# A hybrid decoder layer on one core: the memory of the output product is laid out anew, and the last token tile takes its contraction halves in another order

## What is computed

```
xn     = rmsnorm(x)
merged = gate0 * (att @ w_att_out) + gate1 * (ssm @ w_ssm_out) + gate2 * (mem @ w_mem_out)
h      = x + merged @ w_o                      # w_o is 1024 x 1024: "the output product"
hn     = rmsnorm(h)
h      = h + hier_moe(hn)                      # top-1 group of 4, then top-2 of its 8 experts
y      = rmsnorm_final(h)
```

## Time and profile before

| what | value |
|---|---|
| median of 3 runs | 1182.9 us (1180.64 to 1184.21) |
| the profiled execution | 1183.2 us, of which the span from first to last instruction is 1181.5 us |
| PE busy / weight loads | 1066.9 us (90%) / 761.1 us (64%) |
| DVE / ACT / POOL busy | 35% / 19% / 11% |
| DMA | 330.32 MB, mean 280 GB/s; 412 to 424 GB/s in most slices of the second half |

### The profile page before, as it was taken

How to read it: one execution, slowest core, us unless ns; L and a number is a source line. 1 busy time by engine, 2 the same in 40 slices (tenths; PEclk the granted TensorE clock), 3 DMA queues, 4 the chain that set the end, 5 groups by cost and what they waited for, 6 DMA issues and landing times.

```text
span 1181.5 us, 16647 instructions
## 1 busy us (share of the span) xinstructions
PE 1066.9 (90%) x6831; PEld 761.1 (64%) x6831; DVE 412.2 (35%) x869; ACT 227.1 (19%) x445; POOL 135.1 (11%) x153
## 2 busy tenths in 40 slices
PE   7999999999999999999999599987887787888885
PEld 6888888887888888878845355544444444444441
DVE  3993305926566655422543510100000000000003
ACT  4103021125232222410032201111101111111114
POOL 2113401003010100000010011110011111110100
PEclk9999999999999999999999799999999999999998
DMA  6771266434766645279084499999999999999974
GB/s 229 248 263 55 90 226 229 136 113 169 231 227 229 219 158 188 93 280 395 34 313 169 173 412 392 415 418 420 417 418 421 420 420 421 424 421 419 418 316 148
DMA packets 50812, 330.32 MB, mean 280 GB/s; under 512 B 9084, under 2 KB 12236, under 8 KB 37552
## 3 DMA queue, kind: packets, MB, share of 16 engines
q1 hardware_dynamic: 33760, 259.75, 54.9%
q0 software_dynamic: 15104, 63.85, 16.3%
q10 hardware_dynamic: 1872, 5.66, 1.3%
HBM read 319.18 MB, written 62.11 MB: 323 GB/s over the span
## 4 chain that ended last, share of the span: by engine, by line
PE 64%; DMA 31%; ACT 2%; issue 1%; DVE 1%; SPq 1%; POOLq 0%; ACTq 0%; DVEq 0%
DMA arena<-in_w 26%; PE bank L777 14%; PE bank L957 12%; PE bank L1308 8%; PE bank L1171 5%; PE bank L1333 4%; PE bank L1162 4%; DMA arena<-in_w_stream 2%; PE bank L1081 2%; PE bank L869 2%; PE bank L790 1%; PE bank L948 1%; PE bank L996 1%; PE bank L1017 1%; ACT arena L1588 1%
## 5 line engine op out<-in xcount | busy, mean ns | idle before, releaser
L1308 PE MATMUL bank<-arena 128*64 128x256 f32 x2048 | 261.3, 411 | 64.9 <-DMA arena<-in_w 64.8
L1308 PEld LDWEIGHTS bank<-arena 128*64 128x64 f32 x2048 | 160.2, 143 | 157.9 <-issue 51.0
L777 PE MATMUL bank<-arena 128*128 128x260 f32 x768 | 169.8, 383 | 0.6 <-DMA arena<-in_w_stream 0.6
L777 PEld LDWEIGHTS bank<-arena 128*128 128x128 f32 x768 | 145.5, 190 | 23.3 <-issue 1.0
L957 PE MATMUL bank<-arena 128*128 128x260 f32 x672 | 152.6, 384 | 1.7 <-DVE arena L1913 1.7
L957 PEld LDWEIGHTS bank<-arena 128*128 128x128 f32 x672 | 125.7, 190 | 22.0 <-DVE arena L1913 2.5
L2244 DVE TENSOR_TENSOR arena<-arena,bank 128x256 f32<-128x256 f32 x32 | 13.5, 421 | 326.7 <-ACT arena L1645 326.7
L1333 PE MATMUL bank<-arena 128*64 128x512 f32 x512 | 117.2, 600 | 3.9 <-DVE arena L2250 3.0
L733 POOL DMA_INDIRECT y_dram<-arena,scatter_rows x31 | 44.3, 1428 | 385.6 <-ACT arena L1661 355.2
L1333 PEld LDWEIGHTS bank<-arena 128*64 128x64 f32 x512 | 37.3, 138 | 64.9 <-issue 55.6
L1645 ACT ACTIVATE arena<-bank 128x256 f32<-128x256 f32 x32 | 12.3, 383 | 318.9 <-PE bank L1308 318.9
(11 more groups left out here) (356 smaller groups left out, 1123.8 us busy)
## 6 DMA issues: line engine op xcount, KB each, us to landing
arena<-in_w SPq DMA_DIRECT2D x95, 2048.0 KB, 35.7
arena<-in_w_stream SPq DMA_DIRECT2D x50, 512.0 KB, 5.1
out_sample_swa_k<-in_cache_swa_k POOLq DMA_DIRECT2D x8, 2047.0 KB, 9.6
out_sample_swa_v<-in_cache_swa_v POOLq DMA_DIRECT2D x8, 2047.0 KB, 10.0
arena<-in_cache_mem_v SPq DMA_DIRECT2D x8, 512.0 KB, 8.2
arena<-in_w_o SPq DMA_DIRECT2D x2, 2048.0 KB, 9.9
out_sample_swa_k<-in_cache_swa_k POOLq DMA_DIRECT2D x8, 511.0 KB, 5.9
out_sample_swa_v<-in_cache_swa_v POOLq DMA_DIRECT2D x8, 511.0 KB, 5.7
```

The lines of the kernel that those rows point to most:

```text
L777: last = pe.matmul(bank[:, 2 * u + h, 0:HALF], ring[u][:, k, :], x[:, k, h * HALF:(h + 1) * HALF], start=k == 0, stop=k == KT - 1)
L1308: last = pe.matmul(bank[64 * q:64 * q + CAP, 2 + u, part * FE // 2:(part + 1) * FE // 2], xgT[e // 2 % 2][:, k, 64 * u:64 * u + CAP], w[:, ...
```

## The change

The homes of the weights are laid out anew, so that a seventh home (75.25 KB) is free during the product. For that `xh` has two buffers where it had three, `hnb` one where it had two, `scrap` goes (the squares are written into `hnb`, which holds the normed rows of the tile before, so that ACT waits for their store, `hnst`, ahead of L1612), and `w_o` is loaded in four pieces, one after another, once the branch products are through. The last tile takes k = 4 to 7 for both halves of the columns first (quarters 0 and 1) and k = 0 to 3 after that (quarters 2 and 3); the second half of `w_o` is then free after quarter 1 (`wo_right`), and n = 7 is loaded into its place. In that tile `turn_half(i, 0)` stands behind quarter 3, and the right half's transposes use another bank. Matrix n = 8 is loaded after the last matmul of the product, n = 9 behind the first gather; n = 7 is no longer split. `gain_f` (512 KB) is loaded at the end of the weights where it was loaded ahead of the product.

```
-HOMES = (66, 107.25, 123.25, 139.25, 155.25, 171.25, 50, 91.25, 187.25, 30)
+HOMES = (59.25, 107.25, 123.25, 139.25, 155.25, 171.25, 75.25, 187.25, 91.25, 30)
...
-        w_o = [at(HOMES[6], 4, D), at(HOMES[8], 4, D)]
-        xh = [at(30 + 4 * i, D) for i in range(3)]
-        hnb = [at(42, D), at(MK + 16.25, D)]
+        w_o = [at(kb, D) for kb in (38, 42, 46, 50.25)] + [at(HOMES[7] + 4 * k, D) for k in range(4)]
+        xh = [at(30 + 4 * i, D) for i in range(2)]
+        hnb = at(MK + 16.25, D)
...
-            sp.dma_start(w_o[1], t["w_o"][:, 4:8, :]).then_inc(s["wo"], 16)
             sp.wait_ge(s["Sj"], KT)
-            sp.dma_start(w_o[0], t["w_o"][:, 0:4, :]).then_inc(s["wo"], 16)
-            sp.dma_start(gain_f, t["norm_f"].partition_broadcast(P)).then_inc(s["gainf"], 16)
-            for i in range(3):
+            for k0, n in ((0, 2), (2, 1), (3, 1), (4, 4)):
...
+                sp.dma_start(dst, src).then_inc(s["wo"], 16)
+            for i in range(2):
                 load_x(i)
...
-            for i in (3, 4):
-                sp.wait_ge(hacc[i % 3], 16)
-                sp.wait_ge(s["hn"], i - 2)
-                sp.wait_ge(s["ht"], 2 * (i - 2))
+            for i in range(2, NT):
+                sp.wait_ge(hacc[i % 2], 16 * (i // 2))
+                sp.wait_ge(s["hn"], i - 1)
+                sp.wait_ge(s["ht"], 2 * (i - 1))
                 load_x(i)
-                for n in ((2, 3, 4), (5,))[i - 3]:
+                for n in ((2, 3), (4, 5), (6,))[i - 2]:
                     load_weight(n // 3, n % 3)
...
+            sp.wait_ge(*later("wo_right", 1))
+            load_weight(2, 1)
             sp.wait_ge(s["wo_mm"], 2 * NT - 1)
-            load_weight(2, 0)
+            load_weight(2, 2)
+            sp.wait_ge(hnst, 16 * NT)
             for i in range(2):
-                sp.wait_ge(hnst[i], 16 * len(range(i, NT, 2)))
-            load_half(0)
-            for i in range(3):
-                sp.wait_ge(hacc[i], 16 * len(range(i, NT, 3)))
+                sp.wait_ge(hacc[i], 16 * len(range(i, NT, 2)))
             sp.wait_ge(s["ht"], 2 * NT)
             sp.wait_ge(s["xg"], 16)
-            load_half(KT // 2)
-            load_weight(2, 2)
             load_weight(3, 0)
             for n in range(NHOME, NLOAD):
                 wait_release(n // 3, n % 3)
                 load_weight(n // 3, n % 3)
 
+            sp.dma_start(gain_f, t["norm_f"].partition_broadcast(P)).then_inc(s["gainf"], 16)
...
-                for k in range(4 * (quarter % 2), 4 * (quarter % 2) + 4):
+                ks = list(range(4 * (quarter % 2), 4 * (quarter % 2) + 4))
+                opens, closes = quarter % 2 == 0, quarter % 2 == 1
+                if i == NT - 1:
+                    half, opens, closes = quarter % 2, quarter < 2, quarter >= 2
+                    ks = range(4, 8) if opens else range(4)
+                for k in ks:
...
-                if quarter % 2 == 1:
+                if closes:
                     last.then_inc(s["wo_mm"], 1)
+                elif i == NT - 1 and quarter == 1:
+                    last.then_inc(later_sem("wo_right"), 1)
...
                 out_rows(i, 2)
-                turn_half(i, 0)
+                if i < NT - 1:
+                    turn_half(i, 0)
                 slot_tokens(i - 2)
                 out_rows(i, 3)
+                if i == NT - 1:
+                    turn_half(i, 0)
                 rank(i - 1)
...
                 act.wait_ge(s["h"], 2 * i + 1)
-                act.activation(scrap[0][0:n, :], x[0:n, 0:512], ACT.Square, accum_out=stat[0:n, 32 + i:33 + i]
+                wait_from(act, hnst, 16 * i)
+                act.activation(hnb[0:n, 0:512], x[0:n, 0:512], ACT.Square, accum_out=stat[0:n, 32 + i:33 + i]
                                ).then_inc(s["hss"], 1)
...
                 act.wait_ge(s["rstd"], i + 1)
-                wait_from(act, hnst[i % 2], 16 * (i // 2))
-                act.activation(hnb[i % 2][0:n, :], x[0:n, :], ACT.Copy, scale=stat[0:n, 5 + i:6 + i]
+                act.activation(hnb[0:n, :], x[0:n, :], ACT.Copy, scale=stat[0:n, 5 + i:6 + i]
                                ).then_inc(s["hn"], 1)
```

More of the change, by code:

```diff
@@ L103 @@
 END_BANK = (0, 2, 4, 6, 0)
-SPLIT = tuple(16 if i == 7 else 0 for i in range(NHOME))
 LATE = 29
@@ L340, in build @@
         xgT = [at(XN + 8, KT, P), at(XN + 12, KT, P)]
-        hT = [at(XN + 16, 2, P), at(86, 2, P)]
-        xg = at(82, D)
-        gain_f = at(46, D)
+        hT = [at(XN + 16, 2, P), at(58.25, 2, P)]
+        xg = at(54.25, D)
+        gain_f = at(50.25, D)
         sg = [at(MK + 16.25 + i, FE // 2) for i in range(2)]
@@ L372, in build @@
         wld = [sem(f"s_wld{i}") for i in range(NHOME)]
-        rows_in = [sem(f"s_rows_in{i}") for i in range(3)]
-        hacc = [sem(f"s_hacc{i}") for i in range(3)]
-        hnst = [sem(f"s_hnst{i}") for i in range(2)]
+        rows_in = [sem(f"s_rows_in{i}") for i in range(2)]
+        hacc = [sem(f"s_hacc{i}") for i in range(2)]
+        hnst = sem("s_hnst")
         def h_back_in(T):
-            return (rows_in[T], 16 * (len(range(T, NT, 3)) + 1)) if T < 3 else \
+            return (rows_in[T], 16 * (len(range(T, NT, 2)) + 1)) if T < 2 else \
                 (kdec[T], 32 * len(range(T, NB, NSLOT)) + 16)
@@ L706, in _ @@
                 pool.wait_ge(s["h"], 2 * i + 2)
-                pool.dma_start(h_acc[T * P:T * P + n, :], xh[i % 3][0:n, :]).then_inc(hacc[i % 3], 16)
+                pool.dma_start(h_acc[T * P:T * P + n, :], xh[i % 2][0:n, :]).then_inc(hacc[i % 2], 16)
                 pool.wait_ge(s["hn"], i + 1)
-                pool.dma_start(t["hn_dram"][T * P:T * P + n, :], hnb[i % 2][0:n, :]).then_inc(hnst[i % 2], 16)
+                pool.dma_start(t["hn_dram"][T * P:T * P + n, :], hnb[0:n, :]).then_inc(hnst, 16)
             pool.wait_ge(s["xgclear"], 1)
+            pool.wait_ge(hnst, 16 * NT)
             for i in range(2):
-                pool.wait_ge(hnst[i], 16 * len(range(i, NT, 2)))
-            for i in range(3):
-                pool.wait_ge(hacc[i], 16 * len(range(i, NT, 3)))
+                pool.wait_ge(hacc[i], 16 * len(range(i, NT, 2)))
             def one_pass(p, late=0):
@@ L1169, in out_rows @@
                 T, half = ORDER[i], quarter // 2
-                for k in range(4 * (quarter % 2), 4 * (quarter % 2) + 4):
+                ks = list(range(4 * (quarter % 2), 4 * (quarter % 2) + 4))
[4 more added lines that the diff above has]
+                for k in ks:
                     last = pe.matmul(bank[:, 2 * (i % 2) + half, :], gates[:, k, T * P:T * P + P],
-                                     w_o[k // 4][:, k % 4, half * 512:(half + 1) * 512],
-                                     start=k == 0, stop=k == KT - 1)
-                if quarter % 2 == 1:
+                                     w_o[k][:, half * 512:(half + 1) * 512],
+                                     start=opens and k == ks[0], stop=closes and k == ks[-1])
+                if closes:
                     last.then_inc(s["wo_mm"], 1)
+                elif i == NT - 1 and quarter == 1:
+                    last.then_inc(later_sem("wo_right"), 1)
             def turn_half(i, half):
@@ L1179, in turn_half @@
                 pe.wait_ge(s["h"], 2 * i + half + 1)
-                if half:
+                b = 2 if half and i == NT - 1 else 4
+                if half and b == 4:
                     pe.wait_ge(s["htA"], i + 1)
@@ L1184, in turn_half @@
                 for k in range(4):
-                    last = pe.transpose(bank[:, 4, k * P:k * P + n],
-                                        xh[i % 3][0:n, (4 * half + k) * P:(4 * half + k + 1) * P], ident[0:n, 0:n])
+                    last = pe.transpose(bank[:, b, k * P:k * P + n],
+                                        xh[i % 2][0:n, (4 * half + k) * P:(4 * half + k + 1) * P], ident[0:n, 0:n])
                 last.then_inc(s["ht"], 1)
@@ L1223, in _ @@
                     last = pe.matmul(bank[32 * q:32 * q + NB, 0, 0:256], gates[:, k, SEQ:TOK],
-                                     w_o[k // 4][:, k % 4, q * 256:(q + 1) * 256],
+                                     w_o[k][:, q * 256:(q + 1) * 256],
                                      start=k == 0, stop=k == KT - 1, skip_group_check=True)
@@ L1618, in _ @@
                 act.wait_ge(s["h"], 2 * i + 2)
-                act.activation(scrap[1][0:n, :], x[0:n, 512:D], ACT.Square, accum_out=stat[0:n, 37 + i:38 + i]
+                act.activation(hnb[0:n, 512:D], x[0:n, 512:D], ACT.Square, accum_out=stat[0:n, 37 + i:38 + i]
                                ).then_inc(s["hss"], 1)
@@ L1635, in _ @@
             act.wait_ge(s["hss"], 3 * NT)
-            act.activation(scrap[0][:, 0:1], scrap[0][:, 0:1], ACT.Silu).then_inc(s["hss"], 1)
+            act.activation(stat[:, 63:64], eps_ap, ACT.Silu).then_inc(s["hss"], 1)
             def one_pass(p, late=0):
@@ L2166, in _ @@
```

(3 more changed lines are left out.)

33 lines of the change are left out of this document (15 added, 18 removed).

## The result

| | before | after |
|---|---|---|
| median of the runs | 1182.59 us (4 runs) | 1198.74 us (1197.61 to 1199.15, 4 runs) |
| the profiled execution, its span | 1183.2 us, 1181.5 us | 1198.66 us, 1197.0 us |

The ratio of after to before is 1.0136, 95% interval 1.0118 to 1.0153: 16 us slower, outside the range given (1177 to 1189).

A forecast was written before the change was run, and what follows sets the result against it. PE and then the store and gather bound the time before the experts, DMA bytes the later stream; -1.3 + 2.4 + 0 - 0.3 - 0.6 + 0.5 = +0.7 gave a median of 1183.6 us, range 1177 to 1189.

The forecast's parts named there:

- The bound and the early bytes: Before n = 15: PE sets its release, the queue runs dry, so early loads save 1.3 us (0 to 2.7) of 7.9.
- The first rank: Rank after tile 1: PE waits for the store of tile 0's normed rows; +2.4 us, bounds 1.3 to 3.9.
- The wait here is nearer to the 1.88, and I count no fall: PE's clock was taken to hold behind the first rank's wait; a fall, 1.5 us, stood only in the upper bound.
- Tiles 2 to 4: Later stores of normed rows were taken to land before ACT's squares need the buffer; 0 us, bounds 0 to +3.2.
- The rival: Tile 1's store lands late beside loads, and PE waits 3.2 us more at one rank; 1186.8 us, chance 0.24.
- the sum of all bounds: All terms at their limits together, before the experts and at the end: -4.1 to +6.8 us.
- The later ones meet fewer loads: Stores of normed rows after tile 1's were taken to have fewer loads beside them, within the term of 0 us.
- the prediction's own signs of being wrong: Queue still working when n = 15 goes, PE idle at a second rank, or last load earlier than expert 1's `down` moved.
- The last tile: End of the product: new order shifts store and slot tables; -0.3 us (-0.5 to +1.6), and the gather -0.6 (0 to -2.2).
- The slot tables come at 672.3, which the slack of 672.84 - 670.74 = 2.1 covers: Behind the product: slot tables 1.6 us later were taken not to delay the first gather, given 2.1 us of slack.
- Two `xh`, w_o in pieces: Row and `w_o` loads in the product arrive in time; 0 us, though a late row load would cost 3 to 8.
- `gain_f`: Its load at the end of the weights, behind n = 95 beside the last scatter, costs +0.5 us (0 to +1.3).

The follow-up runs named there:

- the loads behind the store's landing: The changed kernel, but SP issues rows and weights of tiles 3 and 4 only once the competing store of normed rows has landed; 1184.21 us, ratio 1.0017.
- behind its issue: The changed kernel, but SP issues rows and weights of tiles 3 and 4 right behind POOL's issue of the competing store; 1184.71 us, ratio 1.0019.
- both tries with PE kept busy: The changed kernel with extra matmuls ahead of the second and third rank: 14 (experts given other rows), 1190.26 us; then 7 in another bank, 1193.80 us.
- one `hnb` in the kernel before: The kernel before with a single `hnb`, squares written into it, L1612 waiting for the store, loads as before; 1187.23 us, ratio 1.0040.
- Routing first: The changed kernel with squares in their own place, and in the last tile DVE routes tile 3 before adding the left half; 1178.99 us, ratio 0.9969.

## Why the prediction was wrong

*The bound and the early bytes: right.* PE paces the product, and SP's queue is empty when n = 15 goes, which `down` of expert 1 still releases. The term was -1.3 with a bound of -2.7; the landing of n = 15 gives -3.0, a little beyond the bound. So the backlog that n = 15 saw by its landing was saved in full, not by half, and of the 7.9 us of early bytes the rest was lost, as said.

*The first rank: the wait right, the clock wrong.* 2.43 us was measured for +2.4. The step that failed is "The wait here is nearer to the 1.88, and I count no fall": the quarter behind it cost 1.7 us more. I judged from the distance to two rows. Of the six traces with a wait of 2.4 to 2.5 us at this rank the clock fell in five: the kernel after (5.38 us for the next quarter), the loads behind the store's landing (5.04) and behind its issue (5.34), and both tries with PE kept busy (6.66 and 5.38). It did not with one `hnb` in the kernel before (3.68 behind 2.41). Such a wait should have had the fall in its sum, not only in its bound; the price there, 1.5, was near.

*Tiles 2 to 4: the step that failed and cost most.* "I take it as in time: 0" with "n = 4 and 5 follow when the store of h that stands ahead of it on POOL's queue has landed". That store had landed by then: SP's gate is the later of it and the normed rows, and it was the normed rows. SP then issues 0.24 us ahead of POOL. The store of tile 1 took 10.0 us, against the 6.05 that it had, and PE waited 3.9. The rival had this mechanism, with 3.2 us at one rank; the sum of all bounds, +6.8, leaves these 3.2 out. What no case had is the second place: "The later ones meet fewer loads" holds for the last store (3.2 us) but not for tile 2's, which meets the rows of tile 4 and n = 6 in the same way, since the change deals the loads anew over three tiles. PE standing still at a second rank was among the prediction's own signs of being wrong. Two waits of 3.9 and their two slow quarters, 2.5 and 2.4, make 12.8 us, and the runs with the loads behind the store take 13.8 to 14.1 back.

That packets of two queues alternate on a DMA engine (the Trainium skill, DMA: Bandwidth & Descriptors, section Queues, rings and completion order) agrees with a store that loads slow down, and with the 22 packets of either queue in one microsecond. It doesn't tell how much the order of issue matters: 10.0 us at 0.24 behind, 5.8 at 0.1 ahead, 2.9 alone.

*The last tile: mis-sized.* Counted from the end of the last quarter, the store landed 0.4 us earlier than before (-0.3 was said), and the gather took 4.57 us, 0.5 less (-0.6 was said). What failed is "The slot tables come at 672.3, which the slack of 672.84 - 670.74 = 2.1 covers": the tables came 3.8 later, not 1.6 (656.9 + 5.4 is 662.3, not 662.4, which changes nothing). DVE's delay made 2.0 of it, and the transposes and the router at the lower clock (1.11 for 0.66 us, 3.47 for 2.03) the rest. So the gather went out 2.0 later, and for -0.3 and -0.6 it was +1.5. Routing first takes 2.1 back.

*Two `xh`, w_o in pieces:* in the waits of PE and DVE from 560 to 685 none is put down to their loads, as said (the pieces of w_o were issued from 547.1 and first used at 589.1). *`gain_f`:* +0.5 was not confirmed; +0.6 is the whole rest at the end, and moving it gave nothing.

## What to carry to other kernels

When a buffer is saved by letting an engine wait for a store, ask what is issued at the moment of the store: a transfer released by the same event on another queue can go first and make the store three times as long; order the two by hand. A wait of 2 to 4 us of PE, where it paces a stage, is to be counted with the slow clock that may follow, here 6.6 us on 10.3. And bytes brought early are worth only what the queue would otherwise not have had time for: see which wait releases the next transfer before counting them.

## What the runs showed of the hardware

A store of 512 KB took 2.9 to 3.3 us alone, 5.8 when its issue began 0.1 us ahead of the loads of 4.5 or 2.5 MB, and 10.0 when it began 0.24 us behind such loads. Behind them it moved as many packets as the loads, but of 4 KB where theirs had 16 KB. Behind PE's waits of 2.4 to 2.5 us the granted clock fell in five of six traces, and the next quarter took 5.0 to 6.7 us for 3.7; behind the two of 3.9 in the kernel after it fell both times, and the next quarter took 6.1 to 6.2. Filling 3.2 us of such a wait with matmuls kept the clock where 0.91 us of standing still was left, and did not where 2.10 was left. A short wait is not safe by itself: in the kernel after the clock was down behind waits of 1.00 and 0.76 us at the end of the product.
